# Thirty-two stationary columns in place of 128 for the sample's level products of a chunked recurrence

## The reference, cut to what matters

```python
def hgrn2_chunk(S, inp):
    q, k, v, g = inp                       # g: log of the forget gate
    b = jnp.cumsum(g, axis=2)
    o = jnp.einsum('bhtk,bhkv->bhtv', q * jnp.exp(b), S)        # what the state gives
    ...
    decay = jnp.exp(jnp.minimum(bs[:, :, :, :, None] - bs[:, :, :, None, :], 0.0))
    diag = jnp.einsum('bhaik,bhajk,bhaijk->bhaij', qs, ks, decay) * tri
    scores = off + jnp.einsum('bhaij,ac->bhaicj', diag, jnp.eye(n, dtype=diag.dtype))
    o = o + jnp.einsum('bhts,bhsv->bhtv', scores.reshape(bn, h, c, c), v)
    ...
    return S_new, o
```

## Time and profile before

| | |
|---|---|
| median of 3 runs | 2337.89 us (2335.49 to 2340.64) |
| the profiled execution | 2339.31 us |
| its span, first to last instruction | 2337.6 us |
| TensorE matmuls (PE) busy | 2296.9 us, 98% |
| TensorE weight loads (PEld) busy | 2269.3 us, 97% |
| VectorE busy | 1250.9 us, 54% |
| ScalarE busy | 1027.2 us, 44% |
| mean granted TensorE clock | 0.996 |

### The profile page before, as it was taken

The page is one execution under the profiler, slowest core; times in us unless marked ns, Lnnn a source line. Parts: engine busy times, 40 slices in busy tenths (PEclk is TensorE's granted clock), DMA queues, the critical chain, the costliest instruction groups (busy, mean ns, idle before and its releaser), DMA issues. The chain is left out here.

```text
span 2337.6 us, 45540 instructions
## 1 busy us (share of the span) xinstructions
PE 2296.9 (98%) x18073; PEld 2269.3 (97%) x18073; DVE 1250.9 (54%) x2213; ACT 1027.2 (44%) x1418; POOL 101.8 (4%) x105
## 2 busy tenths in 40 slices
PE   7999999999999999999999999999999999998999
PEld 6999999999999999999999999999999999997998
DVE  6444444444444444433257777777777777776221
ACT  5444444444444444533244444444444444444221
POOL 6000000000000000211000000000000000003000
PEclk9999999999999999999999999999999999998999
DMA  7322223223222222244532222222222222212542
GB/s 237 100 86 86 86 86 86 86 86 86 84 83 83 85 85 86 76 115 131 153 92 77 75 75 75 76 77 78 78 76 75 75 75 75 75 48 73 139 116 79
DMA packets 388088, 211.29 MB, mean 90 GB/s; under 512 B 9091, under 2 KB 378294, under 8 KB 388022
## 3 DMA queue, kind: packets, MB, share of 16 engines
q1 hardware_dynamic: 340182, 181.19, 27.3%
q10 hardware_dynamic: 47872, 29.64, 4.2%
HBM read 186.41 MB, written 24.38 MB: 90 GB/s over the span
## 5 line engine op out<-in xcount | busy, mean ns | idle before, releaser
L481 PE MATMUL psum<-act_hi,w_hi 128*128 128x272 f32 x5120 | 1080.1, 292 | 12.3 <-DVE act_lo L1475 6.1
L481 PE MATMUL psum<-act_hi,w_lo 128*128 128x272 f32 x5120 | 1061.6, 289 | 0.0
L481 PE MATMUL psum<-act_lo,w_hi 128*128 128x272 f32 x5120 | 1058.9, 288 | 0.0
L1170 DVE TENSOR_TENSOR w_lo<-w_raw,w_hi 128x1024 fp32r<-128x1024 f32 x320 | 399.5, 1249 | 822.5 <-ACT w_hi L796 821.0
L481 PEld LDWEIGHTS psum<-act_hi,w_hi 128*128 128x128 f32 x5120 | 804.6, 189 | 15.9 <-DVE act_lo L1475 5.5
L481 PEld LDWEIGHTS psum<-act_lo,w_hi 128*128 128x128 f32 x5120 | 806.9, 189 | 0.0
L481 PEld LDWEIGHTS psum<-act_hi,w_lo 128*128 128x128 f32 x5120 | 802.6, 189 | 0.0
L796 ACT ACTIVATE w_hi<-w_raw 128x1024 fp32r<-128x1024 f32 x320 | 338.0, 1057 | 645.7 <-PE psum L481 591.1
L796 ACT ACTIVATE work<-work 128x544 f32<-128x544 f32 (+2 forms) x368 | 261.4, 723 | 309.5 <-DVE work L1304 192.3
L796 ACT ACTIVATE work<-psum 128x512 f32<-128x512 f32 (+4 forms) x256 | 109.7, 483 | 145.1 <-PE psum L472 111.7
L457 POOL TENSOR_TENSOR act_lo<-full,act_hi 128x544 fp32r<-128x544 f32 x24 | 38.9, 1622 | 1867.8 <-DVE act_lo L1179 1842.7
(11 more groups left out here) (214 smaller groups left out, 1772.6 us busy)
## 6 DMA issues: line engine op xcount, KB each, us to landing
w_raw<-in_w_in SPq DMA_DIRECT2D x256, 512.0 KB, 4.0
w_raw<-in_w_out SPq DMA_DIRECT2D x64, 512.0 KB, 6.5
out<-work ACTq DMA_DIRECT2D x48, 256.0 KB, 2.4
x_residual<-work ACTq DMA_DIRECT2D x32, 272.0 KB, 3.8
work<-x_residual SPq DMA_DIRECT2D x32, 272.0 KB, 2.9
full<-in_x_prompt SPq DMA_DIRECT2D x3, 1024.0 KB, 11.3
work<-in_cache_k ACTq DMA_DIRECT2D x16, 128.0 KB, 2.2
work<-in_cache_v ACTq DMA_DIRECT2D x16, 128.0 KB, 4.1
```

The costliest lines, as they stand in the source:

```text
L481: mm = pe.matmul(acc[par][:, j, :], w[:, slot, k % KH, :], a[:, k, j * HT:(j + 1) * HT], start=(k == 0 and n == 0), stop=(k == KT - 1 and ...
L1170: dve.tensor_tensor(w_lo[:, slot], w_raw[:, slot], w_hi[:, slot].bitcast(F32), ALU.subtract).then_inc(lo_ready, 1)
```

## The change

The stationary operand of the sample's product is cut from 128 columns to the sample's own 32, and the product is written to rows 96 to 127 of PSUM, where these rows stood before. The masked copy on VectorE reads and writes those 32 rows only.

```diff
@@ rec_level (TensorE)
                 if m <= SAMPLE // 2:
                     rhs = x[:, SEQ:T].rearrange("p (b j) -> p b j", j=2 * m)[:, :, m:2 * m]
-                    mm = pe.matmul(M[bank][:, 256:256 + SAMPLE // 2], x[:, LAST:T], rhs, start=True, stop=True)
+                    mm = pe.matmul(M[bank][SROW:P, 256:256 + SAMPLE // 2], x[:, SEQ:T], rhs, start=True, stop=True)
                 mm.then_inc(r_lev, 1)
@@ put (VectorE)
-                    dst = A[:, SEQ:T].rearrange("p (b j) -> p b j", j=2 * m)[:, :, m:2 * m]
-                    src = M[bank][:, 256:256 + SAMPLE // 2].rearrange("p (b j) -> p b j", j=m)
+                    dst = A[SROW:P, SEQ:T].rearrange("p (b j) -> p b j", j=2 * m)[:, :, m:2 * m]
+                    src = M[bank][SROW:P, 256:256 + SAMPLE // 2].rearrange("p (b j) -> p b j", j=m)
                     nb = SAMPLE // 2 // m
-                    ins = dve.copy_predicated(dst, msk[:, 64 // m - nb:64 // m, :], src)
+                    ins = dve.copy_predicated(dst, msk[SROW:P, 64 // m - nb:64 // m, :], src)
```

## The result

The changed kernel takes 2347.34 us (median of 6 runs, 2346.08 to 2348.52) where the kernel before, run beside it, takes 2338.34 us: 9.0 us more, a ratio of 1.0039 with a 95% interval of [1.0026, 1.0052]. The forecast was 12.4 us more. The span of the profiled execution went from 2337.6 to 2346.6 us at the same granted clock, 0.996.

A forecast was written before the change was run, and what follows sets the result against it. TensorE's own pace was taken to bound the loop; per L610, 0.20 + 0.04 + 0.18 = 0.42 us replaces 0.22, and 62 x 0.20 = 12.4 us more gives 2350.3 us against the median, range 2341 to 2363 us.

The forecast's parts named there:

- What bounds the loop: Recurrence's loop: TensorE runs at its own pace, 57.95 us per head; VectorE has 14.7 us per head to spare.
- the gap of 0.31 us: Sign: L610's first load starts some 0.31 us after L606's last, where it was 0.11.
- no new wait: Sign: in the loop TensorE still has no wait once per head; a new wait for `put` would be wrong.
- the full-array load: Sign: the next full-array load starts some 0.22 us after L610's first load.
- Entering: Ahead of L610: TensorE empties on the change of array shape, 0.20 us lost, as before L632.
- First load: L610's first weight load, cut to 32 columns: taken at 0.04 us, between 0.03 and 0.11.
- Second pass with leaving: L610's second pass and return to the full array: 0.18 us, from the 32-row transpose at the kernel's start.
- The last head: Head after the loop's 15: two of its four L610 matmuls charged, the others disappear in TensorE's waits.
- VectorE: Masked copies cut to 32 partitions: shorter (at most 10.8 us over 64) or not, no effect on kernel time.
- No drain for a column tile: Rival at L610: cutting columns doesn't empty TensorE, 0.16 us won each, 9.9 us faster, 2328.0 us; chance 0.11.
- No effect: Rival at L610: drain and savings cancel, or the narrow form runs like the full one, 2337.9 us; chance 0.09.
- The drain with nothing saved: Rival at L610: L632's whole loss, 0.39 us each, 24.2 us slower, 2362.1 us; chance 0.15.

## Why the prediction was right, and where its size was off

**What bounds the loop.** Right: what TensorE's pace lost per head, 0.53 us, the kernel lost per head, and the half of the change that touches VectorE alone moved nothing there. Of the signs that the prediction named, the gap of 0.31 us came and no new wait did; the full-array load came 0.17 us behind the narrow one and not 0.22, and the head is 58.49 us long and not 58.75, both for the term below. One sign failed: VectorE's busy time did not stay at 43.25 us.

**Entering.** Right: 0.20 us over the pace, taken from the row tile of L632, holds for a column tile of 32 and of 64 columns.

**First load.** Taken at 0.04 us between 0.03 and 0.11: measured 0.028. Loads go with the columns: 0.028 us for 32, 0.055 for 64, 0.11 for 128. "TensorE: Matmul & The Clock Gate", LDWEIGHTS, in the Trainium skill has it so; the traces agree.

**Second pass with leaving.** This is the term that was mis-sized. Taken at 0.18 us, from a transpose that loads 128 columns and streams 32; measured 0.137: 0.028 for the load and 0.11 for the way out. Of the transpose's 0.18, its load of 128 columns is 0.11, which leaves 0.07 for its way out, less than L610's 0.11 although it streams twice the columns. So the load was taken 0.08 too long and the way out 0.04 too short: two errors that partly cancelled, by luck, and a transpose was no measure for the way out of this matmul. With the first load that is 0.055 us less than forecast. Another 0.01 us each comes back behind the drain, where the loads start at 0.109 instead of 0.112. So 0.20 became 0.133 us, and 62 x 0.133 = 8.3 us in place of 12.4; the 0.7 us from there to the measured 9.0 are well within the interval, which reaches from 6 to 12 us. The range's lower part was right to reach there; the point lay too high because I took a whole row as a price where its load was known to be of another width.

**The last head.** Charged with two of four; what it lost can't be told. From its L639 to the end of the span it is 2119.44 to 2337.6 us before, 218.2, and 217.6 after. No loss shows there, but executions differ by more than the 0.4 us at stake (216.7 with the matmul alone changed), and in both traces TensorE's granted clock stands at the lower of its two levels, 1.2 GHz, for part of that stretch (0.50 from 2119.44 to 2126 us before, 0.50 from 2128.91 to 2134.8 after; it fell during waits of TensorE of 3.95 and 4.65 us). Ahead of that point, from the loop's last L639 to this one, it is 55.85 us before and 57.56 after:

```profile
2063.59 0.48 PE L639 MATMUL psum<-own_hi,ones_r 128*128 128x512 f32 x1
...
2071.35 0.50 PE L639 MATMUL psum<-own_hi,ones_r 128*128 128x512 f32 x1
...
2128.91 0.79 PE L639 MATMUL psum<-own_hi,ones_r 128*128 128x512 f32 x1 [4.65 <-DVE own_lo L1382]
```

That is 1.7 us more, where four narrow matmuls cost 0.5. It is 57.48 us with the matmul alone changed, but also 57.13 with the copy alone, in one execution each, so the narrow matmul is not the cause of it all. TensorE waits for VectorE there, so the slower copies could reach it; the median with the copy alone shows no such cost (2337.87 us against 2337.81). The cause of these 1.2 us stays open.

**VectorE.** Costed at nothing, right; but I bounded the copies as shorter or unchanged, and their pace got slower (below).

**The rivals.** No drain for a column tile: out, by the gap of 0.31. No effect: out. The drain with nothing saved: out, since the loads shrank and the way out is shorter for 16 columns. The rule that a change of tiling mode drains TensorE is in "TensorEngine Tiling (Array Packing)", Key Properties, of the Trainium skill. These runs agree for column tiles too: 0.20 us ahead of a tile of 32 or 64 columns.

## What to carry to other kernels

A float32 matmul on a part of the array, alone among full ones, paid twice for emptying TensorE in these runs: 0.20 us ahead of it, behind a matmul of 128 columns, and 0.11 to 0.20 us behind it, by how much it streams itself (some 0.07 behind the transpose of the earlier trace rows). Loads of 32 columns instead of 128 give back 0.08 us each. So here the lone small matmul was better on the full array, with more columns than it needs or with rows of zeros. By an estimate, small ones are worth their shape only when more than two stand together: the two in a row took 0.43 us (1259.46 to 1260.00, less the pace of 0.11), and two full ones would take some 0.44, four loads of 0.11. More than two were not tried, nor a change from one part shape to another. In a profile such a place shows as a gap between weight loads, ahead of a form other than 128\*128, with no semaphore to explain it; busy shares hide it.

## What the runs showed of the hardware that was not expected

A VectorE copy on the last 32 partitions, 96 to 127, among instructions on all 128, did not overlap its neighbours. With the copy on 128 partitions (here the kernel with the matmul alone changed), it starts 0.33 us after the start of L1333 and the next instruction 0.08 us after it:

```profile
1254.06 0.43 DVE L1333 COPY_PREDICATED work<-level_mask,psum 128x256 f32<-128x256 int32 x1
1254.39 0.17 DVE L1341 COPY_PREDICATED work<-level_mask,psum 128x16 f32<-128x16 int32 x1
1254.47 0.28 DVE L1317 TENSOR_TENSOR work<-work 128x128 f32<-128x128 f32 x1
```

With the last 32 partitions (the kernel with the copy alone changed), these are 0.46 and 0.21 us:

```profile
1252.45 0.43 DVE L1333 COPY_PREDICATED work<-level_mask,psum 128x256 f32<-128x256 int32 x1
1252.91 0.18 DVE L1341 COPY_PREDICATED work<-level_mask,psum 32x16 f32<-32x16 int32 x1
1253.12 0.29 DVE L1317 TENSOR_TENSOR work<-work 128x128 f32<-128x128 f32 x1
```

The durations hardly moved (0.17 and 0.18 us, against the earlier trace rows); the 0.13 us on each side is the lost overlap at this level (0.25 and 0.17 at level 2), and a head's four copies together add 1.2 us of busy time. Whether it is the number of partitions or where they start was not tried. One record hints at the start: where L632 was widened, the memset of the 96 partitions 0 to 95 begins before the one on 128 ahead of it has ended (1190.43 + 0.51 = 1190.94), so fewer partitions alone don't end the overlap there.

```profile
1190.43 0.51 DVE L1506 MEMSET work<- 128x544 f32 x1
1190.92 0.17 DVE L1507 MEMSET work<- 96x128 f32 x1
```

In the loop the lost overlap cost nothing, because VectorE had 14.7 us per head to spare.
